# Expert dots started two heads behind the top-k choice, and prompt, projection and attention steps moved one unit earlier in a hand-written step plan

## What is computed

```python
mod = silu(cond) @ w_ada + b_ada                      # shift, scale, gate, twice
h = rmsnorm(x, norm_mix) * (1 + scale1) + shift1
hq, hff, hfb, hi, hgt, cq, ckv, kpe = split(h @ w_in) # 3,232 columns
o = scan_forward(hq, hff, hi) + scan_backward(hq, hfb, hi)      # gated linear recurrence, 8 heads
hg = rmsnorm(o, hgrn_norm) * silu(hgt)
attn = attend(rmsnorm(cq) @ wqb, keys and values of rmsnorm(ckv) @ wkvb)   # 8 heads
x = x + gate1 * (concat(hg, attn) @ w_out)
h2 = rmsnorm(x, norm_ffn) * (1 + scale2) + shift2
s1, s2 = scores of h2 @ peer_wq against two sets of 128 sub-keys, for 8 heads
idx, gate = the 16 best of the 16 x 16 sums of the best s1 and s2, per head
x = x + gate2 * sum_k(softmax(gate)_k * gelu(h2 . peer_u[idx_k]) * peer_v[idx_k])
```

## Time and profile before

| | us |
|---|---|
| median of 3 runs (5006.93 to 5011.45) | 5008.91 |
| the profiled execution | 5006.78 |
| its span in the trace | 5004.5 |
| DVE busy | 2901.0 (58%) |
| PE busy | 3174.2 (63%) |
| POOL busy | 2810.7 (56%) |
| DMA moved | 1610.48 MB, mean 322 GB/s |

### The profile page before, as it was taken

The page is one execution under the profiler, slowest core; times in us unless marked ns, Lnnn a source line. Parts: engine busy times, 40 slices in busy tenths (PEclk is TensorE's granted clock), DMA queues, the critical chain, the costliest instruction groups (busy, mean ns, idle before and its releaser), DMA issues. The chain is left out here.

```text
span 5004.5 us, 51288 instructions
## 1 busy us (share of the span) xinstructions
PE 3174.2 (63%) x18926; PEld 1961.4 (39%) x18926; DVE 2901.0 (58%) x7102; ACT 582.1 (12%) x1275; POOL 2810.7 (56%) x2565
## 2 busy tenths in 40 slices
PE   6746987735676576568467955784557657657136
PEld 5542834524424423525333753343431441441001
DVE  1348675178547647673873469514874774784750
ACT  2201012201001001101111011220100100100000
POOL 0006672017667667755875644331667767767776
PEclk9677997766896797789689976897579779679569
DMA  6447894239999999989998976674799999999999
GB/s 222 158 143 266 360 357 168 71 119 355 410 419 341 407 419 353 385 357 376 362 405 346 376 296 194 223 256 160 265 403 417 345 418 418 339 419 418 350 406 371
DMA packets 447494, 1610.48 MB, mean 322 GB/s; under 512 B 55312, under 2 KB 57744, under 8 KB 445584
## 3 DMA queue, kind: packets, MB, share of 16 engines
q0 software_dynamic: 368640, 1342.34, 69.6%
q1 hardware_dynamic: 78608, 264.88, 14.3%
HBM read 1603.58 MB, written 3.44 MB: 321 GB/s over the span
## 5 line engine op out<-in xcount | busy, mean ns | idle before, releaser
L571 POOL DMA_INDIRECT ring<-in_peer_u,eidx x1280 | 1577.8, 1233 | 1389.9 <-DVE eidx L1394 619.9
L1418 DVE CUSTOM_DVE_ANT_0 ring<-ring,h 128x1024 f32<-128x1024 f32 x1280 | 1532.3, 1224 | 341.0 <-DMA ring<-in_peer_u,eidx 332.8
L571 POOL DMA_INDIRECT ring<-in_peer_v,eidxT x1280 | 1232.6, 963 | 781.3 <-PE acc L861 456.2
L861 PE MATMUL acc<-ring,wz 128*32 128x512 f32 x5120 | 1175.5, 616 | 295.5 <-DMA ring<-in_peer_v,eidxT 285.0
L861 PEld LDWEIGHTS acc<-ring,wz 128*32 128x32 f32 x5120 | 274.3, 111 | 1037.4 <-issue 963.2
L814 PE MATMUL pp<-hT,wring 128*128 128x128 f32 x2560 | 358.1, 303 | 110.6 <-DMA wring<-in_w_q 104.1
L814 PEld LDWEIGHTS pp<-hT,wring 128*128 128x128 f32 x2560 | 337.0, 215 | 138.7 <-DMA wring<-in_w_q 114.5
L613 PE MATMUL tb<-ident,lat 128*128 128x128 f32 (+1 forms) x412 | 103.3, 400 | 354.4 <-DVE lat L1400 269.8
L784 PE MATMUL tb<-U,lat 128*128 128x64 f32 x672 | 150.0, 398 | 232.9 <-ACT lat L901 232.9
L654 PE MATMUL pp<-wring,hT 128*128 128x128 f32 (+1 forms) x2240 | 266.6, 281 | 20.8 <-DMA wring<-in_w_in 15.8
L654 PEld LDWEIGHTS pp<-wring,hT 128*128 128x128 f32 x2240 | 260.7, 197 | 35.2 <-DMA wring<-in_w_in 23.7
(11 more groups left out here) (199 smaller groups left out, 3369.7 us busy)
## 6 DMA issues: line engine op xcount, KB each, us to landing
wring<-in_w_q SPq DMA_DIRECT2D x160, 512.0 KB, 6.7
wring<-in_w_in SPq DMA_DIRECT2D x125, 512.0 KB, 6.6
wring<-in_w_ada SPq DMA_DIRECT2D x96, 512.0 KB, 6.4
wring<-in_w_out SPq DMA_DIRECT2D x80, 512.0 KB, 6.7
ring<-in_peer_u,eidx POOLq DMA_INDIRECT x1280, 7.2
ring<-in_peer_v,eidxT POOLq DMA_INDIRECT x1280, 7.2
wqb<-in_wqb SPq DMA_DIRECT2D x4, 1152.0 KB, 9.4
wkvb<-in_wkvb SPq DMA_DIRECT2D x4, 1024.0 KB, 6.4
```

The lines of the kernel that those rows point to most:

```text
L571: pool.indirect_dma_start(ring[:, n % GR, :], None, A[table], bass.IndirectOffsetOnAxis(ap=rows, axis=0),).then_inc(s_g[n % GR], 16)
L861: ins = nc.tensor.matmul(acc[32 * q:32 * q + 32, half * 512:(half + 1) * 512], wz[:, at:at + 32], row[:, half * 512:(half + 1) * 512], sta ...
L1418: v.tensor_tensor_reduce(rows, rows, h2[:, u % 2, :], 1.0, 0.0, ALU.mult, ALU.add, dot[:, n:n + 1])\
```

## The change

Six things change in the order of the steps.

1. `chosen_and_read` lays the dots of a unit behind its choice by two heads: heads 0 and 1 are chosen, then eight chunks of head 0 go between the choices of heads 1 and 2, and so on. It is used for units 0, 1 and 6, whose choice stood alone. The last 16 chunks follow.
2. `keys_values` is split: scan-state products (`hgo`, once part of `hgfin`) come first, then transposes, keys, values, and the output norms last. The latent norms (`latn`) go to the end of the projections, with a step of their own for their two row loads (`rows`).
3. `tile` is split into `attention` and `queries`; the load of the sub-keys is a step of its own (`keys`) between them.
4. At the start, the modulation tiles 24 to 47 are laid beside keys and attention, tiles 16 to 23 alone beside the scan.
5. The work is laid out anew over the units: attention of units 3 and 4 and the queries of unit 3 beside unit 2's dots, the queries of units 2 and 7 beside the value sums of units 1 and 6, the second prompt pass (unit 5) complete by the end of unit 3's value sums, projections of latent layer 1 beside unit 4's dots, its first three scans beside unit 4's value sums, the fourth tile beside unit 5's dots. Six of the 26 projection tiles of layer 0 move from unit 0's dots to its value sums.
6. To allow this, the second batch of projections reads its own copy `hT1` of the normed input, and the waits on shared buffers are adapted.

```diff
+def projections(p, b, lo=0, hi=N_IN):
+    out = [(("inp", p, b, j), 2 * max(1, (t1 - t0) * 0.9)) for j in range(lo, hi)]
     if hi == N_IN:
+        out.append((("fgate", p, b), 4))
+        out += [(("small", p), 0)] if b == 0 else []
+        out += [(("rows", p), 0), (("latn", p), 3 + 3 * NT[p])] if b == len(BATCHES[p]) - 1 else []
...
 def keys_values(p):
-    out = [(("hgS", p), 5)] if PASSES[p][0] else []
-    out += [(("hgfin", p, t), 4) for t in range(nt)]
-    return out + [(("latn", p), 3 + 3 * nt), (("latT", p), 3 * nt), (("kn", p), 10 * big), (("va", p), 4 * big)]
+    out = [(("wb", p), 0)]
+    if g:
+        out += [(("hgS", p), 5)] + [(("hgo", p, t), 2) for t in range(nt)]
+    out += [(("latT", p), 3 * nt), (("kn", p), 20 if g else 6), (("va", p), 9 if g else 2)]
+    return out + [(("hgfin", p, t), 4) for t in range(nt)]
...
+def chosen_and_read(p, t, beside):
+    u = U0[p] + t
+    heads = choice(p, t)
+    share = TOPK // CU
+    out = [heads[0], heads[1]]
+    for hh in range(2, H):
+        out += [(("u", u, c), 2.6) for c in range((hh - 2) * share, (hh - 1) * share)] + [heads[hh]]
+    return spread(out + [heads[H]], beside), [(("u", u, c), 1) for c in range((H - 2) * share, NCU)]
...
-    out += spread(scans(0, 0, 1), last)
-    out += [step for step, _ in keys_values(0) + tile(0, 0) + choice(0, 0)]
-    beside_u = {0: projections(1, 0), 4: keys_values(2) + tile(2, 0),
-                5: projections(3, 0, 13) + projections(3, 1) + scans(3, 0, 2)}
-    beside_v = {0: scans(1, 0, 4), 4: choice(2, 0) + projections(3, 0, 0, 13),
-                5: scans(3, 2, 4) + keys_values(3) + tile(3, 0)}
-    after = {0: keys_values(1) + tile(1, 0) + choice(1, 0), 5: choice(3, 0)}
-    for p in (1, 3):
-        for t in range(1, NT[p]):
-            beside_u[U0[p] + t - 1] = tile(p, t)
-            beside_v[U0[p] + t - 1] = choice(p, t)
-    beside_v[1] = spread(beside_v[1], modulations(1, 0, N_ADA // 2))
-    beside_v[2] = spread(beside_v[2], modulations(1, N_ADA // 2, N_ADA))
-    beside_v[3] += projections(2, 0) + scans(2, 0, 1)
+    out += spread(scans(0, 0, 1), modulations(0, 2 * SECT, 3 * SECT))
+    out += spread(keys_values(0) + attention(0, 0), modulations(0, 3 * SECT, N_ADA))
+    entry = {0: (0, 0, norms(1, 0) + projections(1, 0, 0, 16)), 1: (1, 0, []), 6: (3, 0, [])}
+    ahead = {1: keys_values(1) + attention(1, 0) + [(("keys", 1), 0)] + queries(1, 0)}
+    beside_u = {0: projections(1, 0, 16, 20), 1: attention(1, 1),
+                2: attention(1, 2) + attention(1, 3) + queries(1, 2),
+                3: keys_values(2) + attention(2, 0) + [(("keys", 1), 0)] + queries(1, 3),
+                4: norms(3, 0) + projections(3, 0),
+                5: norms(3, 1) + projections(3, 1) + scans(3, 3, 4) + keys_values(3)[:6],
+                6: attention(3, 1), 7: attention(3, 2) + queries(3, 2), 8: attention(3, 3) + queries(3, 3)}
+    beside_v = {0: projections(1, 0, 20) + scans(1, 0, 4),
+                1: queries(1, 1) + spread_pairs(choice(1, 1), modulations(1, 0, N_ADA // 2)),
+                2: modulations(1, N_ADA // 2, N_ADA) + choice(1, 2) + norms(2, 0) + projections(2, 0) + scans(2, 0, 1),
+                3: choice(1, 3) + [(("keys", 2), 0)] + queries(2, 0) + choice(2, 0),
+                4: scans(3, 0, 3), 5: keys_values(3)[6:] + attention(3, 0) + [(("keys", 3), 0)] + queries(3, 0),
+                6: queries(3, 1) + choice(3, 1), 7: choice(3, 2), 8: choice(3, 3),
+                9: [(("y", u), 3) for u in range(NU - 5, NU - 1)]}
```

## The result

The changed kernel took 5046.77 us (median of 4 runs, 5038.53 to 5051.25) against 5009.67 us of the kernel before in the same runs (4 runs, 5006.93 to 5011.45): a ratio of 1.0073, 95% interval 1.0055 to 1.0090. That is 37 us slower. It lies in the range 4890 to 5085 and in forecast A's own 4970 to 5050, but not at its point: the sum said +5. The profiled execution took 5051.25 us (span 5049.4), the longest of the four, and 44 more than the profiled one of before.

The account below looks back on a forecast made before the run. No engine was taken to bound the kernel, so it was read stretch by stretch. Gains of 300 us and losses of 305 gave net +5 on the profiled 5006.8, so 5012 us, range 4890 to 5085.

Parts of the forecast that it names:

- forecast A: Whole kernel: work is moved, not hidden; choices' alone time is bought with longer sums; 4970 to 5050 us, chance 0.45.
- 23 tiles at 2.2 us, 51: Unit 2's value sums: modulation columns ahead of the choice add 51 us, within 271 us against 197, +74.
- At transfers' pace: Unit 4's value sums 170 us against 211, -41; unit 5's dots at 370 GB/s, 222 against 300, -78.
- Start ... 0: Start of the kernel: left at 0 change, as it has the same bytes or the same steps.
- Unit 0's sums: Six moved projection tiles (44 us), gates and latent norms (13 us) ahead of scans: 237 us against 180, +57.
- unit 1's sums: Queries moved beside them, then eight heads with modulation tiles between: 245 us against 196, +49.
- the norms behind the keys: Stretch before unit 1: output norms follow the value copies, not hidden beside keys; stretch changes by -9 us.
- the -92: Entries of units 0, 1 and 6: dots behind the choice remove DVE's waiting; -54, -18 and -20 us.
- -20 and +39: Unit 6: entry 274 us against 294, -20; value sums with the moved queries 204 against 165, +39.
- B: Rival, faster: chains beside sums and dots run at the transfers' pace; 4900 us, chance 0.30.
- C: Rival, slower: ten buffers against sixteen dots make each of 18 entry rounds wait 4 us; +72, 5085 us, chance 0.15.
- D: Rival: early dots gain nothing as POOL holds gathers until after the choice; entry gain only -45, 5060 us, chance 0.10.

Follow-up runs that it names:

- Experiment 2: Changed kernel with the modulation columns mixed again with the heads' choices beside unit 2's value sums: 5014.14 us, ratio 1.0018 to the kernel before.
- experiment 3: Changed kernel with the start's modulation tiles 16 to 47 beside the first scan again, keys and attention without them: 5021.71 us, ratio 1.0035 to before.
- experiment 4: Changed kernel with the scan's output norms again ahead of transposes, keys and values, state products still apart: 5036.85 us, ratio 1.0072 to before.
- Experiment 1: Changed kernel with the choices of units 0, 1 and 6 alone again, ahead of their dots: 5074.33 us, ratio 1.0153 to the kernel before.
- experiments 1 and 5: The second: changed kernel with unit 6's choice alone and unit 7's queries beside unit 6's dots again: 5018.57 us, ratio 1.0011 to before.
- experiment 8: Changed kernel with unit 5's queries mixed with unit 4's choice beside unit 3's value sums: 5003.89 us, ratio 0.9995 to the kernel before.
- the combination: Changed kernel with units 1, 6 and start as before, unit 2's and 3's sums mixed; slow-transfer chips only: 5131.2 us (0.9760 to before), 5124.3 us (0.9724).

## Why the prediction was right or wrong

**Mechanism A held**: work was moved, not hidden. Nine of the 16 stretches came within 10 us, and the median fell into A's own range, near its upper end. That is partly the width of the range: the chances leaned to faster (0.46, against 0.40 for slower). The point of 5012 was 35 us under the median and 39 under the profiled execution, which it was meant for, through sizes: three stretches whose chains I made too short, and two that I called transfer-bound.

**"23 tiles at 2.2 us, 51" was too small.** Measured: 65 us from the dots' end to the first head. I took the landing of a sparser pattern, three tiles in flight, as the whole price. In those 65 us, with 22 gathers issued, PE was busy for 50.66, with the value sums and the columns' own products, and waited for tiles besides:

```profile
PE pp L886 <- DMA wring<-in_w_ada: 13.4, 11, 1.9
```

Product and landing add up here, where the term had the landing alone. The other 6 of the 20 lie in choice, projection and scan, 78 + 101 + 47 = 226 us against the 228 - 8 allowed. Experiment 2 shows that 23 us of this were due only because columns and choice stood in a row.

**"At transfers' pace" was too small twice.** Unit 4's sums: 181 instead of 170, at 380 GB/s and not 418. Unit 5's dots: 238 instead of 222. Their two halves in the windows of the changed kernel:

```profile
2966.00:3100.00 134.00, 62.33 (x456) 57.41 (x456) 101.86 (x206) 17.60 (x44) 86.02 (x72) 0.78 0.96 371
3100.00:3204.00 104.00, 36.49 (x300) 33.44 (x298) 101.93 (x179) 6.56 (x12) 74.67 (x55) 0.50 0.82 285
```

The first runs at 371 GB/s, the 370 I had assumed for the whole; in the second DVE is busy for 101.93 of 104 us, with scan work and dots, and transfers drop to 285. So DVE looks like the bound of the second half; that is read from the profile, and no run tested it.

**"Start ... 0" was wrong**: 13 us in the profile, 9 on the mean of nine, of which experiment 3 gives 5 to 9 to the modulation tiles that now stand between the steps of keys and attention. "The same bytes" says nothing of that order.

**Unit 0's sums**, 248 for 237: six tiles plus latent norms ahead of the scans cost 68, above the upper bound of 65. From the first of the six tiles to the end of the last it is 58 us, and not the 44 of the tiles by themselves, as the value sums stand between them and the last, narrow one took 10.3:

```profile
592.30 7.83 PE L703 MATMUL pp<-wring,hT 128*128 128x128 f32 x64
...
640.45 10.30 PE L703 MATMUL pp<-wring,hT 128*128 128x32 f32 x64
```

**Too long were** unit 1's sums (234 for 245) and unit 5's (254 for 266). Both counted further chunks beside a chain of PE at two thirds of 1.84 us each; no run tested that share. Two bounds were added up wrongly, without effect on the point: the entries at DVE's busy time would be -170 and not -155, and the transfers alone of units 1 and 6's sums +50 for the pair and not +25.

**Right as worked out**: unit 0's entry (254 for 256), unit 2's dots, unit 3's sums; the norms behind the keys, not beside them (experiment 4); a gap before unit 2's first head. Unit 1's entry was 10 us better than forecast, 3 to 8 in the other profiles: dots behind one another start 1.15 us apart, not 1.23 (below), and no allowance for the ring was needed.

**The reason given for the -92 was half wrong.** I laid the gain of units 1 and 6 to DVE's waiting that goes away with the early dots. Experiment 1 shows 0 to 9 us for that; the other 23 (292 to 269) and 16 (294 to 278) come of the queries leaving the stretch, and experiments 1 and 5 together show that in unit 6 they cost 33 us more in their new place than in the old. The prediction had this loss in its terms (-20 and +39), but laid the gain to something else.

**The rivals.** B fell: the sums of units 2, 3 and 5 run at 313 to 321 GB/s and unit 2's dots at 319, not at the 418 of transfers. Only the sums of units 1 and 6 came nearer (393 and 381). C fell: gathers in the entry landed 5.9 us after issue, as this row of the DMA issues of the changed kernel between 1049 and 1313 us shows, and DVE's waits for `ring` there summed to 0.9 us.

```profile
ring<-in_peer_u,eidx POOLq DMA_INDIRECT x128, 5.9
```

D fell as a mechanism: POOL issued the first gather of unit 1 at 1059.5 us, behind the first head's row numbers, and went on through the choice of the next. Its size for units 1 and 6 was nearly true all the same, for another reason: DVE was full with or without the early dots.

**Where the gain went.** Gains of 303 us (entries 105, before unit 1 6, unit 4's sums 30, unit 5's dots and sums 154, dots of 3 and 4 8) stand against losses of 346: sums of unit 2 94, of unit 0 68, of 6 48, of 3 40, of 1 38, dots of unit 2 45, start 13. One at a time, by the ratios against 1.0073, mixing unit 2's columns is worth 28 us, mixing unit 3's queries 39, undoing unit 6's part 31, the start 19, and unit 0's part nothing; any of the first three is about the whole loss of 37.

**Open**: why experiment 8 gave 33 and not 60, what besides the start's 5 to 9 us gained in experiment 3, unit 5's dots, and the combination on a chip of the usual transfers.

## What to carry to other kernels

Where every engine walks one list of steps, count a stretch as the longest chain that stands in a row, and before moving work into a stretch see whether the two engines alternate there: columns, choice and projection, independent of one another, cost 291 us in a row and 268 with only the first two mixed. Work taken from a place where it looks exposed is not gained before its new place is costed with its neighbours; unit 7's queries left an entry for 15 us and came back for 48. Starting a dependent stage early on the engine that is already full gives only the waits, 0 to 9 of some 270 us here; it gave 25 where work of another engine could start with it (unit 0).

## What the runs showed of the hardware

The kernel before differs by 5% between chips (5005 and 5271 us). For the changed kernel two profiles show where: of the 175 us between their spans (5049.4 and 5224.2) 170 lie in the ten stretches of value sums. Bare value sums move the same bytes in 165 us at 418 GB/s or in 192 at 367, while the dots of unit 4, at 380 and 381 GB/s, take 208 us on both chips. There the change itself was no loss (0.9968). That a chain costs less beside sums of 192 us than beside 166 would explain it, but there is no profile of the kernel before from that chip.

A dot shows as 1.22 us and yet they start 1.15 us apart, the second under the end of the first, in DVE's timeline of the changed kernel:

```profile
1068.88 1.22 DVE L1475 CUSTOM_DVE_ANT_0 ring<-ring,h 128x1024 f32<-128x1024 f32 x1
1070.03 0.08 DVE L1475 DVE_READ_ACCUMULATOR2_ANT dot<- 128x1 f32 x1
1070.03 1.22 DVE L1475 CUSTOM_DVE_ANT_0 ring<-ring,h 128x1024 f32<-128x1024 f32 x1
```

So the mean of the group overstates what a row of dots occupies, by 0.07 us a dot, 9 for 128.
